# Who issues the copies of the expert table v, and where

## The reference, cut to what matters

```
def peer_ffn(h, wq, subkeys, u_tab, v_tab):
    ...                                       # two top-16 searches give e: 128 experts of 16384 for each token
    act = jax.nn.gelu(jnp.einsum('thkd,td->thk', u_tab[e], xt))
    return jnp.einsum('thk,thkd->td', g * act, v_tab[e])

for l in range(DEPTH):                        # DEPTH = 2
    ...                                       # h = modulate(x); p = h @ w_in; attention, rwkv, conv; @ w_out; norm
    x = layer_norm(ALPHA * x + g2 * peer_ffn(h, peer_wq, peer_subkeys, peer_u, peer_v), ln2_g, ln2_b)
```

## Time and profile before

| | |
|---|---|
| median of 3 runs | 3725.42 us |
| profiled execution, its span | 3726.81 us, 3725.0 us |
| PE, DVE, ACT busy | 73%, 51%, 25% of the span |
| DMA | 1340.75 MB, mean 360 GB/s |
| SyncE's queue (q1) | 123.99 MB |
| ScalarE's queue (q10) | 409.09 MB |
| GpSimd's queue (q0, the gathers) | 805.36 MB |
| project, layer 0 and 1 | about 104 to 278.5 us, 1936 to 2113 us |
| attention | 278.5 to 380, 2113 to 2223 |
| rwkv | 380 to 661, 2223 to 2497 |
| output | 661 to 737, 2497 to 2576 |
| scoring | 737 to 849, 2576 to 2687 |
| experts | 849 to 1907, 2687 to 3705 |

### The profile page before, as it was taken

The page is one execution under the profiler, slowest core; times in us unless marked ns, Lnnn a source line. Parts: engine busy times, 40 slices in busy tenths (PEclk is TensorE's granted clock), DMA queues, the critical chain, the costliest instruction groups (busy, mean ns, idle before and its releaser), DMA issues. The chain is left out here.

```text
span 3725.0 us, 36147 instructions
## 1 busy us (share of the span) xinstructions
PE 2730.9 (73%) x12342; PEld 1691.5 (45%) x12342; DVE 1901.9 (51%) x4344; ACT 939.6 (25%) x2400; POOL 889.3 (24%) x810
## 2 busy tenths in 40 slices
PE   4776688593777888888757767877757777777775
PEld 2675578591222333333227656867712222222222
DVE  1214644578854444445551236554887555555555
ACT  1334433341111111111123344333311111111111
POOL 0001000002443444344410100000044444444442
PEclk7897799796999999999979868988879999999998
DMA  8997599786999999999979876996689999999995
GB/s 347 372 415 270 210 362 328 277 297 268 420 420 420 417 419 419 418 410 420 420 283 408 344 276 224 355 344 261 230 336 419 419 420 418 414 420 415 420 416 247
DMA packets 249735, 1340.75 MB, mean 360 GB/s; under 512 B 31178, under 2 KB 33738, under 8 KB 139218
## 3 DMA queue, kind: packets, MB, share of 16 engines
q0 software_dynamic: 110592, 805.36, 52.3%
q10 hardware_dynamic: 112192, 409.09, 29.3%
q1 hardware_dynamic: 26772, 123.99, 8.6%
HBM read 1195.69 MB, written 276.86 MB: 395 GB/s over the span
## 5 line engine op out<-in xcount | busy, mean ns | idle before, releaser
L1865 PE MATMUL acc<-exp_uv,exp_diag 128*128 128x512 f32 x3072 | 1432.8, 612 | 559.0 <-ACT exp_diag L1834 558.7
L1734 DVE CUSTOM_DVE_ANT_0 exp_uv<-exp_uv,h_tok 128x1024 f32<-128x1024 f32 x768 | 940.8, 1226 | 906.6 <-DMA exp_uv<-uv_rows,exp_eid 904.5
L1701 POOL DMA_INDIRECT exp_uv<-uv_rows,exp_eid x768 | 850.6, 1107 | 2103.3 <-PE acc L1865 1099.6
L1865 PEld LDWEIGHTS acc<-exp_uv,exp_diag 128*128 128x128 f32 x3072 | 566.9, 193 | 1413.3 <-issue 1413.1
L1843 ACT ACTIVATE exp_gel<-exp_dot 128x2 f32<-128x2 f32 x384 | 78.0, 203 | 1623.8 <-DVE exp_dot L1734 1623.8
L313 ACT COPY rows<-rows_bank 128x512 f32<-128x512 f32 x512 | 276.6, 589 | 508.6 <-PE rows_bank L298 279.5
L298 PE MATMUL rows_bank<-ident,rows 128*128 128x128 f32 x2048 | 292.9, 290 | 104.5 <-ACT rows L313 104.5
L298 PEld LDWEIGHTS rows_bank<-ident,rows 128*128 128x128 f32 x2048 | 243.9, 149 | 145.5 <-issue 142.5
L1834 ACT ACTIVATE exp_diag<-ident,exp_w 128x128 f32<-128x128 f32 x768 | 259.9, 385 | 0.3 <-issue 0.2
L562 PE MATMUL project_bank<-project_hs,project_ws 128*128 128x384 f32 x960 | 189.2, 354 | 23.5 <-DVE project_hs L550 23.5
L562 PEld LDWEIGHTS project_bank<-project_hs,project_ws 128*128 128x128 f32 x960 | 177.6, 200 | 24.1 <-DVE project_hs L550 24.1
(11 more groups left out here) (295 smaller groups left out, 2508.4 us busy)
## 6 DMA issues: line engine op xcount, KB each, us to landing
rows<-in_u ACTq DMA_DIRECT2D x256, 512.0 KB, 8.6
uv_rows<-in_v ACTq DMA_DIRECT2D x256, 512.0 KB, 9.5
uv_rows<-rows ACTq DMA_DIRECT2D x256, 512.0 KB, 8.7
ring<-in_w_ada SPq DMA_DIRECT2D x48, 1024.0 KB, 8.9
ring<-in_w_in SPq DMA_DIRECT2D x20, 1024.0 KB, 8.8
ring<-in_wq SPq DMA_DIRECT2D x16, 1024.0 KB, 8.3
exp_uv<-uv_rows,exp_eid POOLq DMA_INDIRECT x768, 11.6
ring<-in_w_out SPq DMA_DIRECT2D x8, 1024.0 KB, 13.4
```

The costliest lines, as they stand in the source:

```text
L1701: nc.gpsimd.indirect_dma_start(buffer_of(n)[:, :], None, uv_rows, bass.IndirectOffsetOnAxis(eid[:, t, k:k + 1], 0)).then_inc(c.landed[land ...
L1734: V.tensor_tensor_reduce(buffer_of(n)[:, 0:D], buffer_of(n)[:, 0:D], h_tok[:, t, :], 1.0, 0.0, ALU.mult, ALU.add, dot[:, j % 8, n % G:n % ...
L1865: ins = nc.tensor.matmul(acc[2 * t + h][:, :], diag[:, n % DIAGS, :], buffer_of(n)[:, D + 512 * h:D + 512 * h + 512], start=(k == 0), stop ...
```

## The change

The copies of v go from ScalarE to SyncE, and from half pieces to whole ones: one transfer of 1 MB in place of two of 512 KB. They no longer stand beside the turned rows but at set places. Of a layer's 64 pieces SyncE issues 8 in `project` (2, 2, 1, 1, 1, 1 behind its six refills), 14 in `attention` (behind the stores of keys and values), 14 in `rwkv` behind the loads of states and 18 more once the first direction's states are stored, and 10 in `output` behind the gates and the last norm row, ahead of the stores of x. None is issued in `scoring`. The count that `rows_end` waits for is halved, as there are half as many transfers.

```diff
+JOIN_PROJECT, JOIN_ATT, JOIN_RWKV, JOIN_OUT = (2, 2, 1, 1, 1, 1), 14, (14, 18), 10
...
-def rows_join(c, act, m):
-
-    j = m % NK
-    act.dma_start(c.uv_rows[m // 2, :, m % 2, 1, :], c.dram["v"][m // NK, j // 2, :, (j % 2) * D:(j % 2 + 1) * D]).then_inc(c.joined, 16)
+def rows_join(c, sp, count):
+
+    r = c.rows
+    for a in range(r.by_join, r.by_join + count):
+        sp.dma_start(c.uv_rows[a, :, :, 1, :],
+                     c.dram["v"][2 * a // NK, a % (NK // 2)].rearrange("p (two n) -> p two n", two=2)).then_inc(c.joined, 16)
+    r.by_join += count
...
         if m + ROWS_IN < r.end:
             rows_load(c, act, m + ROWS_IN)
-        rows_join(c, act, m)
...
-    act.wait_ge(c.joined, 16 * c.rows.end)
+    act.wait_ge(c.joined, 16 * c.rows.end // 2)
...  (project)
-                refill(c, s, sp, l, AT_IN, N_PIN - SLOTS)
+                for n, pairs in enumerate(JOIN_PROJECT):
+                    refill(c, s, sp, l, AT_IN, n + 1, n)
+                    rows_join(c, sp, pairs)
...
-def refill(c, s, sp, l, first, count):
+def refill(c, s, sp, l, first, end, start=0):
-    for m in range(count):
+    for m in range(start, end):
...  (attention, behind the stores of keys and values)
+                rows_join(c, sp, JOIN_ATT)
                 sp.wait_ge(S["k_stored"], 32)
...  (rwkv)
                 for d in range(2):
+                    rows_join(c, sp, JOIN_RWKV[d])
                     if d == 1:
...  (output)
                 load_row(c, l, sp, S["x_in"], gb[1], "ln1", 1)
+                rows_join(c, sp, JOIN_OUT)
                 for t in range(TILES):
```

More of the change, by code:

```diff
@@ L258, in rows_buffers @@
     r.by_pe = r.by_act = r.first
+    r.by_join = r.first // 2
     c.rows = r
```

## The result

The changed kernel takes 3748.77 us (median of 4 runs, 3740.76 to 3752.83), the kernel before 3725.53 us (4 runs, 3720.67 to 3726.07): a ratio of 1.0058, interval 1.0045 to 1.007. The forecast was 3662 us, in a range of 3632 to 3713. The changed kernel is slower, and the time lies outside the range.

A forecast was written before the change was run, and what follows sets the result against it. Project was taken as bound by transfers at 414 GB/s. Gains of 31 (project), 6 and 4 (attention), 10 (rwkv) and 12 (output) sum to 63 us, taking the profiled 3726.8 to 3664, forecast as 3662 us, range 3632 to 3713.

The forecast's parts named there:

- ceiling of 414 GB/s: All stages: the 16 engines' rate in the middle of project, at share 1.02, was taken as the limit everywhere.
- find some 3 MB of free room: Start of project: the four early pieces, 4.2 MB, mostly fit unused transfer room; 4.4 us of stalls left per layer.
- 212 are left: Rwkv's second direction: rows need 202 GB/s, leaving 212 for 18 pieces, 18.9 MB lasting 89 us, to about 630.
- Project, -31: Project, both layers: fewer bytes remove most stalls, 31 us gained of a possible 40, between 23 and 40.
- if block 7 comes no earlier than now: Project's lower bound: block 7 stays at 171.65 us, later pairs run undisturbed, 23 us gained in both layers.
- Attention, -10: Attention, both layers: 6 us from earlier stores of keys and values, 4 from ScalarE no longer issuing v.
- I cost this at nothing: Attention: 14 added pieces, 14.7 MB at the start, delay no rows, since four loads and three stores stand as buffers.
- Rival A: SyncE's bursts starve ScalarE's rows, -8 us in each layer's attention; 23 us gained in all, 3702 us; chance 0.22.
- Rwkv, -10: Rwkv, both layers: 5 of 7.5 us of ScalarE's store waits go per layer; between -5 and 15 gained.
- Output, -12: Output: first root 6 us earlier per layer, rows at half the ceiling; 12 us in all, between -4 and 19.
- Rival D: One queue's issue blocks the other's while large transfers are outstanding; 103 us slower, 3828 us; chance 0.09.
- The rule against the change: Skill page: any issuer uses the same 16 engines, so moving to SyncE as such is worth only 4 us.

The follow-up runs named there:

- e9: Against e5: 4 pieces (not 0) behind project's first two refills, 5 (not 0) at output's start, 9 in scoring; 3725.95 us, ratio 0.9984.
- e12: The changed kernel with 12 pieces in place of 18 before rwkv's second direction, the other 6 in scoring; 3727.04 us, ratio 1.0001.
- e4: The kernel before, but layer 1 copies no v and reads layer 0's; 3682.99 us, ratio 0.9897.
- e7: The changed kernel with no piece in project, 14 in scoring, 6 after output's last row, attention's and rwkv's partly spread behind rows; 3676.61 us, ratio 0.9868.
- e6: The changed kernel with the same counts per stage but later: project's 8 behind rows 18 to 39, output's 10 after its last row; 3737.24 us, ratio 1.0034.
- e8: The changed kernel with only project's 8 pieces moved later, behind rows 18 to 39; 3732.13 us, ratio 1.0001.
- e3: The kernel before, with whole pieces issued by SyncE, each behind its own second row, so each stage keeps its amount of v; 3735.34 us, ratio 1.0035.
- e5: The changed kernel with no pieces in project or output; those 18 go to scoring, attention and rwkv unchanged; 3689.17 us, ratio 0.9906.
- e11: Against e7: attention's 14 at once, 22 pieces in rwkv's first direction, 6 in its second, 16 in scoring; 3665.93 us, ratio 0.9841.
- e2: The kernel before, with one whole piece behind every second row, still in ScalarE's queue; 3719.12 us, ratio 0.9986.
- e1: The changed kernel with each piece as two 512 KB copies, still SyncE's at the same places; 3738.94 us, ratio 1.004.

## Why the prediction was wrong, point by point

**The step that failed** has two halves. The first is the ceiling of 414 GB/s, "that is the ceiling I use for all stages". It holds for the middle of project before, where rows, v and refills mix. Elsewhere say otherwise in the column beside it, which I didn't divide by: attention 282 / 0.77 = 366, rwkv 294 / 0.81 = 363, scoring 270 / 0.75 = 360, output 288 / 0.73 = 395. After the change the windows of the five stages give 344 to 361, project too (332 / 0.93 = 357). The free part of rwkv was 19%, not the 29% that 294 of 414 seems to leave. The second half is that SyncE's pieces were taken to use only what the rows leave ("find some 3 MB of free room", "212 are left"). They took half, and where rows stood close on TensorE's path, every piece was paid for: 2.0 us from the first one (e9). Two queues of the second direction from 533 to 633 us, before and after (packets, MB, share):
```profile
q10 hardware_dynamic: 9019, 32.84, 92.0%
q1 hardware_dynamic: 288, 0.06, 0.3%
```
```profile
q1 hardware_dynamic: 5055, 18.79, 51.1%
q10 hardware_dynamic: 5100, 18.57, 49.9%
```
Before, it moved 329 GB/s and was 92% full, so some 2.7 MB were free; six more pieces are 6.3 MB. The other 3.6 MB at the 374 GB/s of after are 9.6 us; measured were 8.3 (118.7 - 110.4) in layer 0 and 11.8 in layer 1. This sum gives the size, not the place: the windows under e12 put all of layer 0's loss beside the last eight rows.

**Project, -31, measured -2.8.** The 40 us that project could gain were right (e4, e7). The loss of 4.4 us a layer was not: "the four early pieces find some 3 MB of free room". They found none (e9), and the pieces up to block 7 cost 17.2 us (60.35 - 43.17), those behind it 3.9. Of the 17.2 us, 11.1 are longer waits for rows and 6.1 TensorE's lower clock (42.84 us of work, 36.77 in e7). From block 1 to 19 the prediction had 133.9 us and layer 0 took 149.5. The rate is 8.0 of these 15.6: at 414 GB/s the 21.7 MB up to block 7 would have taken 52.4 us, about as long as before. Nor was "if block 7 comes no earlier than now" a lower bound: it came 9.6 us later. A piece in another queue costs more than its bytes among the rows: from block 1 to 7 of before, the half pieces of 12 rows, the bytes of 6 whole ones, cost 8.0 us (51.15 - 43.17), as much as four of SyncE's. That TensorE can't catch up later was in the text (a pair takes 14.39 us), but it wasn't weighed when the pieces were placed early: stalls early are lost for good, and late pieces cost 0.7 to 1.0 us each (e6, e8).

**Attention, -10, measured -3.2.** VectorE's wait at the start fell by 2.8 us in layer 0, as taken (3), and the 3.0 us of issue waits are gone. But the sign against the forecast came too: ScalarE waits 17.0 and 18.0 us for stores, where there were none. Paced, with 9 pieces (e3), the stage took 97.5 / 102.4 us, 7 and 3 less than with the burst. So "I cost this at nothing" failed as well, and against e3 Rival A's 8 us a layer look near.

**Rwkv, -10, measured +19.9.** About as large a miss as project's 28. "212 are left and 18.9 MB last 89 us, to about 630" was nearly right for the levels, where layer 0 carried twelve pieces at no loss against before. It failed behind 603 us: the sum itself had pieces under way until 630, beside the place "where several rows follow each other", and had no cost for that but a lower bound of -5. The pieces were 18 where 12 had been, and the last of them met the closest rows (e12).

**Output, -12, measured +11.5.** The half share was right: 5.97 of 12.44 MB. The whole was not: 355 GB/s, not 414, so that a row's 1.05 MB take 5.9 us at the half, not 5.1. And before, SyncE had nothing more in its queue from 692.8 on the earlier trace rows, while now its pieces stand there until all rows are done. The text had the last row 37.5 us behind the stage's start; it came 49.9 us behind, and 50.7 with five pieces (e9). Nor were 6 us a layer there to be had: with no v at all in output the stage is 3.9 / 3.7 us shorter (e5). The bound of -4 was not one.

**Rival D** is refuted, in its mechanism and its 3828 us. It is the issuing engine that is held, not the other: SyncE's 14 issues in attention stretch over 40.6 us, while ScalarE's 15 from 278 to 330 us take 0.33 or 0.34 us each. After:
```profile
279.96 40.63 SPq L275 DMA_DIRECT2D uv_rows<-in_v  x14
```
**Rival A** named the mechanism, that ScalarE's rows starve behind SyncE's share, and priced it at 23 us of gain left; right in kind, 47 us short. It had no price for TensorE's clock, and none for rwkv. The slower side had been given only D's price.

**The rule against the change.** The prediction took the move to SyncE as such to be worth the 4 us of issue waits, since three transfers of a row share the engines "whatever their queue". The rows of before can't show that, as all three stood in ScalarE's queue. Measured with the places kept, the move costs 10 us (e3).

## What to carry to other kernels

Divide a window's GB/s by its share before calling the rest room: the ceiling depends on the mix, and a stage at 294 GB/s and 0.81 has 19% free, not 29%. Then ask what the critical engine needs at that moment. TensorE's rows ask for 2.1 MB in 7.2 us in project (291 GB/s) and in 10.4 us in the levels (202 GB/s); half of 360 is 180. A piece of 1.05 MB in the other queue cost 2.0 to 2.5 us early in project, 0.7 to 1.0 late in it, some 2.2 beside the last eight rows of a direction (43.8 us with about 5.5 pieces, 31.8 with none in e4), and 0.3 beside the levels of layer 0 (75.0 us with twelve, 71.5 with none), although the share there was 1.01. That the difference is the rows' own rate is my estimate from these numbers; no run changed it alone. So move such copies by their bytes per stretch (none in the early part of project, few left for the direction's last rows, more in scoring) and ahead of no urgent transfer: that turned +0.6% into -1.6% (e11).

## What the runs showed of the hardware

- The rate at full share depends on what is moved, and how. From 140 to 182 us of project: 412 GB/s at 1.02 with v in ScalarE's queue, 410 with whole pieces there (e2), 401 with whole pieces paced in SyncE's (e3), 382 with halves in bursts (e1), 364 at 0.97 with no v (e7). It is less where v's copies from memory to memory are nearly alone. After, at the start of attention:
```profile
284.00:290.00 6.00, 0.00 (x0) 0.00 (x0) 3.66 (x7) 0.00 (x0) 5.56 (x8) 0.76 1.02 332
290.00:297.00 7.00, 2.84 (x16) 2.80 (x16) 5.59 (x17) 0.00 (x0) 5.80 (x7) 0.50 1.04 282
```
Why one mixture is faster than another stays open.
- A late row costs more than its wait. After TensorE had waited 1.35 and 3.90 us within 7 us, its granted clock fell to the lower of its two levels (1.2 and 2.4 GHz): a row's 8 transposes took 1.94 in place of 1.06 us, and 24 products 5.22 in place of 2.79.
- An engine's own issue is held once several large copies stand in its queue: v's issue on SyncE takes 0.49 us at least, 2.5 in the median and 13.2 at most, and what it issues next lands late (e6). How many may stand there wasn't measured by itself.
- Why a copy in SyncE's queue costs project's rows more than the same bytes in ScalarE's (e3, e9) fits the even turns of the two queues, but no run changed the turns.
